# Inverting the 16x16 diagonal blocks of a delta rule on VectorE by forward substitution, in place of doubled powers on TensorE

## The reference

```python
decay = jnp.exp(jnp.where(causal, gc[..., :, None] - gc[..., None, :], -jnp.inf))
kk = jnp.einsum("nbhcd,nbhed->nbhce", kc, kc)
a_mat = jnp.where(strict, bc[..., :, None] * kk * decay, 0.0) + jnp.eye(CHUNK, dtype=f32)
rhs = jnp.concatenate([vc * bc[..., None], kc * (bc * jnp.exp(gc))[..., None]], axis=-1)
sol = lax.linalg.triangular_solve(a_mat, rhs, left_side=True, lower=True)
...
def step(state, xs):
    v_new = u_n - jnp.einsum("bhck,bhkv->bhcv", w_n, state)
    o = (jnp.einsum("bhck,bhkv->bhcv", q_n * jnp.exp(g_n)[..., None], state)
         + jnp.einsum("bhce,bhev->bhcv", attn_n, v_new))
    state = state * jnp.exp(gl_n)[..., None, None] + jnp.einsum("bhck,bhcv->bhkv", kt_n, v_new)
```

## Time and profile before

| what | us |
|---|---|
| median of 3 runs | 1206.51 |
| lowest and highest | 1205.79, 1206.98 |
| the profiled execution, its own time | 1207.03 |
| its span, first to last instruction | 1205.3 |
| PE busy | 1180.6 (98%) |
| DVE, ACT, POOL busy | 744.6, 597.4, 102.2 |

### The profile page before, as it was taken

One profiled execution on the slowest core, in us unless ns is written; L12 is line 12 of the kernel. 1 busy time (PEld: TensorE's weight loads), 2 busy tenths in 40 slices (PEclk: granted clock), 3 DMA queues, 4 the chain that ended last, 5 costly groups with the idle time before them and its releaser, 6 DMA issues.

```text
span 1205.3 us, 20514 instructions
## 1 busy us (share of the span) xinstructions
PE 1180.6 (98%) x8276; PEld 1100.7 (91%) x8276; DVE 744.6 (62%) x897; ACT 597.4 (50%) x804; POOL 102.2 (8%) x159
## 2 busy tenths in 40 slices
PE   7999999999999999999999999999999999999997
PEld 6998899999888999988999998789999989999875
DVE  5867556555867797763565544565766466554455
ACT  4675444346455675653444433455464355443342
POOL 5310101001010000000000000100400010000011
PEclk8999999999999999999999999999999999999999
DMA  8744343445554675656476555465475548655541
GB/s 223 221 127 153 105 140 106 140 140 198 187 191 140 187 216 174 195 189 187 137 224 195 182 175 195 139 211 172 141 228 191 159 141 268 193 175 175 203 135 63
DMA packets 156019, 208.57 MB, mean 173 GB/s; under 512 B 8608, under 2 KB 127405, under 8 KB 155949
## 3 DMA queue, kind: packets, MB, share of 16 engines
q1 hardware_dynamic: 152781, 198.92, 52.4%
q10 hardware_dynamic: 3072, 8.65, 2.2%
q0 software_dynamic: 96, 0.01, 0.1%
HBM read 206.50 MB, written 1.05 MB: 172 GB/s over the span
## 4 chain that ended last, share of the span: by engine, by line
PE 92%; DVE 3%; ACT 2%; POOL 1%; issue 1%; DMA 1%; POOLq 0%; DVEq 0%; SPq 0%; ACTq 0%
PE ACCP L774 27%; PE ACCP L776 27%; PE ACCP L775 27%; PE SMP L925 3%; PE SMP L918 2%; PE SMP L774 2%; PE SMP L776 2%; PE SMP L775 2%; ACT HI L1399 1%; DVE LO L1899 1%; POOL STAT L651 1%; DMA PRE_GAIN<-in_norm_mix_dram 1%; DVE XS L1935 0%; POOL STAT L650 0%; PE ACCP L895 0%
## 5 line engine op out<-in xcount | busy, mean ns | idle before, releaser
L1899 DVE TENSOR_TENSOR LO<-RAW,HI 128x1024 fp32r<-128x1024 f32 x367 | 437.6, 1231 | 244.9 <-ACT HI L1399 243.8
L1399 ACT ACTIVATE HI<-RAW 128x1024 fp32r<-128x1024 f32 x366 | 368.5, 1053 | 226.9 <-PE ACCP L776 206.1
L774 PE MATMUL ACCP<-XH,HI 128*128 128x256 f32 x1536 | 437.8, 285 | 1.9 <-DVE XL L1944 1.9
L775 PE MATMUL ACCP<-XL,HI 128*128 128x256 f32 x1536 | 435.8, 284 | 0.0
L776 PE MATMUL ACCP<-XH,LO 128*128 128x256 f32 x1536 | 435.8, 284 | 0.0
L774 PEld LDWEIGHTS ACCP<-XH,HI 128*128 128x128 f32 x1536 | 296.0, 193 | 2.3 <-DVE LO L1899 2.2
L775 PEld LDWEIGHTS ACCP<-XL,HI 128*128 128x128 f32 x1536 | 296.0, 193 | 0.0
L776 PEld LDWEIGHTS ACCP<-XH,LO 128*128 128x128 f32 x1536 | 296.0, 193 | 0.0
L774 PE MATMUL ACCP<-HI,HH 128*128 128x512 f32 x264 | 105.0, 398 | 0.0
L776 PE MATMUL ACCP<-HI,HL 128*128 128x512 f32 x264 | 104.6, 396 | 0.0
L775 PE MATMUL ACCP<-LO,HH 128*128 128x512 f32 x264 | 104.6, 396 | 0.0
(11 more groups left out here) (388 smaller groups left out, 1536.0 us busy)
## 6 DMA issues: line engine op xcount, KB each, us to landing
RAW<-in_w_in_dram SPq DMA_DIRECT2D x104, 512.0 KB, 4.4
RAW<-in_w_up_dram SPq DMA_DIRECT2D x44, 512.0 KB, 4.5
RAW<-in_ffn_w_gate_dram SPq DMA_DIRECT2D x44, 512.0 KB, 4.4
RAW<-in_ffn_w_up_dram SPq DMA_DIRECT2D x44, 512.0 KB, 4.6
RAW<-in_ffn_w_down_dram SPq DMA_DIRECT2D x44, 512.0 KB, 4.1
RAW<-in_w_down_dram SPq DMA_DIRECT2D x22, 512.0 KB, 4.1
RAW<-in_w_out_dram SPq DMA_DIRECT2D x8, 512.0 KB, 4.2
RAW<-in_w_mkv_dram SPq DMA_DIRECT2D x8, 512.0 KB, 5.0
```

Of the source, the lines that this page charges most:

```text
L774: pe.matmul(dst, lhs[0], rhs[0], start=start, stop=False)
L775: pe.matmul(dst, lhs[0], rhs[1], start=False, stop=False)
L1399: act.activation(HI[:, n % RING, half_of(half)], RAW[:, n % RAWS, half, :], ACT.Copy).then_inc(hi_ready, 1)
L1899: dve.tensor_tensor(LO[:, s, c], RAW[:, n % RAWS, half, :], HI[:, s, c].bitcast(f32), ALU.subtract).then_inc(lo_ready[s], 1)
```

## The change

The products Dt to P8 leave PE, with the copies that ACT, DVE and POOL make for them. Instead:

1. SP writes the 64 diagonal 16x16 blocks of L to a scratch tensor in DRAM: 8 DMAs, each of 16 partitions with 8 pieces of 64 bytes. They stand between the loads of foxv.0 and foxv.1.
2. After the load of foxv.1, SP waits for them and loads the scratch tensor into DIAG_L: one block a partition, 64 partitions of 1 KB.
3. DVE waits for that and solves all 64 blocks at once by forward substitution: 15 columns, two operations a column (a product of n x m elements, and a subtraction), n = j + 1, m = 15 - j. Each waits for the one before (`link`). The result in DIAG_T is the transposed inverse.
4. SP stores DIAG_T to a second scratch tensor, loads gate_c.0, and places the blocks into MP with 8 DMAs of 64-byte pieces. PE waits for these (diag_placed) ahead of `T16`.

POOL zeroes MP and sets up DIAG_T, where it built the mask DIAG16 before. The arena, the stretch of SBUF that most tiles share, is declared ahead of the small tensors COL, FCONV, IDENT and so on, so that its start is a multiple of 64 bytes.

```diff
-        DL, MAT, MA, MB, MC, ME, MP = (at(f"delta_{n}", 24 + 4 * i, [P, NT, HEADS, P])
-                                        for i, n in enumerate(["L", "AT", "A", "B", "C", "E", "P"]))
+        DL, MAT, MA, MB = (at(f"delta_{n}", 24 + 4 * i, [P, NT, HEADS, P]) for i, n in enumerate(["L", "AT", "A", "B"]))
+        ME, MP = (at(f"delta_{n}", 44 + 4 * i, [P, NT, HEADS, P]) for i, n in enumerate(["E", "P"]))
+        DIAG_L, DIAG_T, DIAG_TERM = (at(f"diag_{n}", 40 + i, [N_DIAG, 16, 16]) for i, n in enumerate(["L", "T", "term"]))
+        diag_l, diag_t = (nc.dram_tensor(f"scratch_diag_{n}", (NT * HEADS, P // 16, 16, 16), f32) for n in "lt")
...
-            load_t("foxv", w["w_in"], C_FV)
+            for j in range(2):
+                load("foxv", Turn(j), t_block(w["w_in"], C_FV, j))
+                if j == 0:
+                    for t in range(NT):
+                        small_is_taken(sp, f"kk{t}")
+                    for g in range(P // 16):
+                        sp.dma_start(diag_l[:, g, :, :].rearrange("q r c -> r q c"), diagonal(DL, g)).then_inc(diag_written, 16)
+            sp.wait_ge(diag_written, 16 * (P // 16))
+            sp.dma_start(DIAG_L[:, :, :].rearrange("b r c -> b (r c)"), diag_l[:, :, :, :].rearrange("q g r c -> (q g) (r c)")).then_inc(diag_loaded, 16)
+            sp.wait_ge(diag_solved, 1)
+            sp.dma_start(diag_t[:, :, :, :].rearrange("q g c r -> (q g) (c r)"), DIAG_T[:, :, :].rearrange("b c r -> b (c r)")).then_inc(diag_stored, 16)
...
+                    if g == "c" and j == 0:
+                        sp.wait_ge(diag_stored, 16)
+                        sp.wait_ge(diag_zeroed, 3)
+                        for i in range(P // 16):
+                            sp.dma_start(diagonal(MP, i), diag_t[:, i, :, :].rearrange("q c r -> c q r")).then_inc(diag_placed, 16)
...
-            for t in range(NT):
-                pe.wait_ge(D_ready, t + 1)
-                turn_four(f"Dt{t}", lambda h: MA[:, t, h, :])
-            t_half("foxqk", 0, XH, XL)
-            for t in range(NT):
-                small_is_taken(pe, f"Dt{t}")
-                four(f"D2_{t}", lambda h: (MB[:, t, h, :], MA[:, t, h, :]))
...
+            for j in range(3):
+                t_half("foxqk", j, XH, XL)
...
-            for t in range(NT):
-                small_is_taken(pe, f"P8_{t}")
+            pe.wait_ge(diag_placed, 16 * (P // 16))
+            for t in range(NT):
                 turn_four(f"T16_{t}", lambda h: MP[:, t, h, :])
...
+            dve.wait_ge(diag_loaded, 16)
+            dve.wait_ge(diag_zeroed, 3)
+            for j in range(15):
+                n, m = j + 1, 15 - j
+                below = DIAG_L[:, n:16, j:n].rearrange("b r o -> b o r").broadcast_to([N_DIAG, n, m])
+                solved = DIAG_T[:, 0:n, j:n].broadcast_to([N_DIAG, n, m])
+                rest = DIAG_T[:, 0:n, n:16]
+                link(dve.tensor_tensor(DIAG_TERM[:, 0:n, 0:m], below, solved, ALU.mult))
+                ins = dve.tensor_tensor(rest, rest, DIAG_TERM[:, 0:n, 0:m], ALU.subtract)
+                if j < 14:
+                    link(ins)
+            ins.then_inc(diag_solved, 1)
```

More of the change, by code:

```diff
@@ L134 @@
 SMALL += ["gTq0", "gTq1", "gTk0", "gTk1", "gTv0", "gTv1", "gcol", "grow0", "grow1", "gFq0", "gFq1", "gFk0", "gFk1"]
-SMALL += ["kk0", "kk1", "kq0", "kq1", "z0", "z1", "z2", "z3", "Dt0", "Dt1", "D2_0", "D2_1", "D2t_0", "D2t_1"]
-SMALL += ["P2_0", "P2_1", "D4_0", "D4_1", "D4t_0", "D4t_1", "rc0", "rc1", "rc2", "rc3", "P4_0", "P4_1"]
-SMALL += ["D8_0", "D8_1", "P8_0", "P8_1", "so0", "so1", "T16_0", "T16_1", "fTq0", "fTq1", "fTk0", "fTk1"]
+SMALL += ["kk0", "kk1", "kq0", "kq1", "z0", "z1", "z2", "z3", "rc0", "rc1", "rc2", "rc3", "so0", "so1", "T16_0", "T16_1", "fTq0", "fTq1", "fTk0", "fTk1"]
 SMALL += ["Z16_0", "Z16_1", "Tt32_0", "Tt32_1", "fS0", "fS1a", "fS1b", "Z32_0", "Z32_1", "T32_0", "T32_1"]
@@ L221, in build @@
         XS = sb("XS", [P, NT, DM])
-        COL = [sb(f"COL{i}", [P, n]) for i, n in enumerate(COL_N)]
-        FCONV = sb("FCONV", [P, CONV_N])
+        ARENA = 86 * 1024
+        arena = sb("arena", [P, ARENA // 4])
+        base = nc.sbuf_base - ARENA
         IDENT = sb("IDENT", [P, P])
@@ L233, in build @@
         TRI = UPTO[:, 0, :]
+        COL = [sb(f"COL{i}", [P, n]) for i, n in enumerate(COL_N)]
+        FCONV = sb("FCONV", [P, CONV_N])
         STAT = sb("STAT", [P, 384])
@@ L374, in build @@
         post_sq, tap_done, dve_mix = sems("post_sq tap_done dve_mix")
+        diag_zeroed, diag_written, diag_loaded, diag_solved, diag_stored, diag_placed = sems(
+            "diag_zeroed diag_written diag_loaded diag_solved diag_stored diag_placed")
         ln_mean, ln_sq, ln_ready = sems("ln_mean ln_sq ln_ready")
@@ L578, in _, with diagonal @@
             load_t("foxqk", w["w_in"], C_FQ)
-            load_t("foxv", w["w_in"], C_FV)
+            def diagonal(m, g):
+                part = slice(16 * g, 16 * g + 16)
+                return m[part, :, :, part].rearrange("r t h c -> r (t h) c")
+            for j in range(2):
[9 more added lines that the diff above has]
+            sp.dma_start(diag_t[:, :, :, :].rearrange("q g c r -> (q g) (c r)"), DIAG_T[:, :, :].rearrange("b c r -> b (c r)")).then_inc(diag_stored, 16)
             for g, branch, wo in (("c", 2, "w_oc"), ("a", 0, "w_oa"), ("b", 1, "w_ob")):
@@ L582, in _ @@
                     load_f("gz", w["w_in"], C_GZ)
-                load_f(f"gate_{g}", w["w_in"], C_GATE + DM * branch)
+                for j in range(4):
+                    load(f"gate_{g}", Turn(j), f_block(w["w_in"], C_GATE + DM * branch + 256 * j))
+                    if g == "c" and j == 0:
[3 more added lines that the diff above has]
+                            sp.dma_start(diagonal(MP, i), diag_t[:, i, :, :].rearrange("q c r -> c q r")).then_inc(diag_placed, 16)
                 for j in range(2):
@@ L723, in _ @@
             pool.memset(ONES, 1.0).then_inc(masks_ready, 1)
+            pool.memset(MP[:, :, :, :], 0.0).then_inc(diag_zeroed, 1)
+            pool.memset(DIAG_T[:, :, :], 0.0).then_inc(diag_zeroed, 1)
+            pool.wait_ge(diag_zeroed, 2)
+            pool.memset(DIAG_T[:, :, :].rearrange("b c r -> b (c r)")[:, 0:256:17], 1.0).then_inc(diag_zeroed, 1)
             lo_of(ON_POOL_CONV)
@@ L729, in _ @@
                 small_is_taken(pool, f"kk{t}")
-                pool.tensor_tensor(MA[:, t], DL[:, t], every(DIAG16[:, :], HEADS), ALU.mult).then_inc(D_ready, 1)
             heads_root(1, 1.0 / DH)
-            for b, last in ((16, "D8"), (32, "Z16"), (64, "Z32")):
+            for b, last in ((16, ""), (32, "Z16"), (64, "Z32")):
                 for t in range(NT):
-                    small_is_done(pool, f"{last}_{t}")
+                    if last:
+                        small_is_done(pool, f"{last}_{t}")
                     pool.tensor_tensor(MA[:, t], DL[:, t], every(LEVEL[b][:, :], HEADS), ALU.mult).then_inc(level_ready, 1)
@@ L1047, in _ @@
                 rest_sums(h)
[L1048 to L1060, removed]
+            for j in range(2):
+                t_half("foxv", j, XH, XL)
             pe.wait_ge(stick_ready, 1)
@@ L2060, in _ @@
             dve.scalar_tensor_tensor(out=SP_[:, :, :], in0=Z[:, :, :], scalar=-1.0, in1=Z[:, :, :], op0=ALU.mult, op1=ALU.max).then_inc(keep_abs, 1)
[L2062 to L2070, removed]
+            dve.wait_ge(diag_loaded, 16)
[10 more added lines that the diff above has]
+            ins.then_inc(diag_solved, 1)
             split_ahead("foxqk", Turn(0))
-            take_small("D2_1", MC[:, 1], by_head(small("D2_1")))
             dve.wait_ge(keep_ln, 1)
@@ L2076, in _ @@
             dve.tensor_tensor(SP_[:, :, SEQ:SEQ + P], SP_[:, :, SEQ:SEQ + P], every(BEFORE[:, :], HEADS), ALU.mult).then_inc(keep_ready, 1)
-            take_small("D2t_1", ME[:, 1], by_head(small("D2t_1")))
             split_ahead("foxqk", Turn(1))
[L2080 to L2088, removed]
             split_ahead("foxqk", Turn(2))
-            take_small("D4t_1", MB[:, 1], by_head(small("D4t_1")))
             def stick_arg(h):
@@ L2101, in _ @@
                 stick_arg(h)
-            for t in range(NT):
-                factor(4, t)
             heads_norm(1, XS, 2 * HW)
             heads_scale(1, lambda t: HT[:, t, :], 8)
-            split_ahead("foxv", Turn(0), (0,))
-            take_small("D8_1", MC[:, 1], by_head(small("D8_1")))
-            split_ahead("foxv", Turn(0), (1,))
+            split_ahead("foxv", Turn(0))
             split_ahead("foxv", Turn(1))
-            for t in range(NT):
-                factor(8, t)
             y_split(0, ("so0", "so1"), lambda g: (YH[:, 2 * g:2 * g + 2, :], YL[:, 2 * g:2 * g + 2, :], by_head(small(f"so{g}"), SEQ)))
```

28 lines of the change are left out of this document (2 added, 26 removed).

## The result

| | median, us | lowest to highest | ratio to before, 95% interval |
|---|---|---|---|
| before | 1206.21 | 1205.79 to 1206.98 | |
| after | 1187.72 | 1186.72 to 1190.55 | 0.9852 [0.9839, 0.9866] |

The account below looks back on a forecast made before the run. TensorE, busy for 98% of the span, was taken as the bound. Gross gain 14.1 less a 0.4 us wait gave 13.7, so 1207.03 became 1193.3, the median 1192.8, stated as 1193.0; range 1191.4 to 1198.0.

Parts of the forecast that it names:

- The shift of the arena costs nothing: Arena's new start: no cost, argued from 512-column operations taking 682 ns on X and XS outside it, 690 on SP_ inside.
- Gross gain 14.1: PE in the delta rule: removed stretches of 13.71 us plus 0.39 for three blocks that follow a block.
- Dt: Removed products ahead of foxqk.0: worth nothing, since the wait there for ACT's copy just grows by about 0.8 us.
- The landing: DIAG_L's load on SP's queue: issued at about 104.9, behind 512 KB landing at 108.3, it lands at 108.9.
- rival 1: The chain is late: landing or solve slips, PE waits 2 to 6 us at rc0, say 4; 1196.5 us, chance 0.20.
- one full small landing more: Upper bound on DIAG_L's landing: 108.3 + 3.8 = 112.1, with a PE wait at rc0 of 3.6 us.
- The solve, 7.2 us: DVE's 30 linked operations at 0.195 us each plus 1.02 ns an element, 1360 elements; bounds 5 and 14 us.
- Rival 2, the column read: DVE reading DIAG_L down a column costs two to four times, solve grows 0.7 to 2.1 us; 1194.2, chance 0.12.
- keep_ready: DVE's signal that PE needs at rc0: comes at 121.6 against PE's arrival at 121.2, a wait of 0.4 us.
- stick_ready: After foxv.1, ACT's exponential ends 5.0 us after foxv.0, foxv.1 covers 5.44: slack 0.4 us, no wait.
- Rivals 3, 4 and 5: Later waits at stick_ready or norms, 1195, 0.07; slow small operations, 1223, 0.05; waits replace PE's removed stretches, 1206.5, 0.03.
- The sum: Whole kernel: gross gain 14.1 less 0.4 of wait at rc0, 13.7 us.

Follow-up runs that it names:

- e5: Kernel before with COL and FCONV declared behind the arena, so the arena has an offset of 0 from HI; 1199.74 us.
- e12: Changed kernel with 96 bytes ahead of its arena, the old offset from HI, so the delta rule's change alone; 1193.62 us.
- e7: Changed kernel with the load of DIAG_L issued ahead of foxv.1 instead of behind it; 1185.38 us.
- e9: Changed kernel with XH and XL 32 bytes off HI and LO, arena at 0 mod 256 from HI, COL0 ahead of the arena; 1176.41 us.
- e11: Changed kernel with XH and XL 64 bytes off HI and LO, arena at 0 mod 256 from HI, COL0 ahead of the arena; 1177.02 us.
- e2: Changed kernel with FCONV declared ahead of the arena, which then starts 32 past a multiple of 64 bytes; 1192.19 us.
- e3: Changed kernel with XH and XL moved to 32 mod 64 by pads, arena then 64 off HI mod 256; 1178.03 us.
- e4: Changed kernel with HI and LO moved to 32 mod 64 by pads, arena then 32 off HI mod 256; 1179.18 us.
- e6: Changed kernel with XH and XL 32 bytes off HI and LO, arena at 128 mod 256 from HI; 1178.64 us.
- e10: e9 plus the load of DIAG_L ahead of foxv.1 and ACT's copy to SV after Z's first half; 1172.28 us.
- e1: Kernel before with FCONV declared behind the arena, which then starts at a multiple of 64 bytes; 1203.65 us.

## Why the prediction was wrong, point by point

**The step that failed most** is the last sentence ahead of the sum: "The shift of the arena costs nothing". It was argued from two rows of DVE, on which the shift indeed does nothing (682 and 691 ns after). But the arena also holds HH, the stationary operand of 792 products of 512 columns, and PE is the engine that bounds the kernel. The missing term is 792 x 7.6 ns = 6.0 us, and 0.67 for the products with MH and YH; e5 measured 6.3, and e12 lies 5.9 above the changed kernel. I costed an edit at nothing by looking at an engine with slack and not at the one without.

**Gross gain 14.1.** Right. From foxqk.0 to the end of the delta rule PE gained 13.55 - 1.85 = 11.7 us with a wait of 2.31 in it, so 14.0 without. Between whole kernels with the same arena offset and no wait: e5 to e7, 1199.74 - 1185.38 = 14.4. Dt was worth nothing, as forecast: the wait for ACT's SV copy grew from 0.62 to 1.57, by 0.95 where 0.8 was said. The three blocks took 16.6 us to the last product's end, against 5.57 + 5.44 + 5.44 = 16.45.

**The landing.** DIAG_L landed at 109.0 and I had said 108.9, but this is luck. All that comes ahead of it ran 1.85 us earlier than in the trace of before. From its own issue the load took 6.1 us, where 108.9 - 104.9 = 4.0 was taken. The mis-sized term is the landing of the half megabyte ahead of it: 4.0 us in the sum, 6.4 measured. The 4.0 is the median of 19 loads, and the sum gave it to one that is not like the median. The trace of before has this very load, the second half of foxv.1, issued at 104.29:

```profile
RAW<-in_w_in_dram SPq DMA_DIRECT2D x1, 512.0 KB, 6.1
```

So "no landing in this stretch is far off its 4.0", with which rival 1 was held small, was a misreading: 104.29 + 6.1 = 110.4, and the wait at rc0 would have come out near 2. The 0.6 us for DIAG_L behind it were 0.2, and the small writes landed after 1.8 and not 3.8, which changed nothing. The bound from above, "one full small landing more", was wide enough. This is rival 1, *the chain is late*, with 2.31 us of wait instead of its 4, one microsecond for one microsecond, as it says.

**The solve, 7.2 us.** 109.03 to 116.33, 7.30. The pitch model (0.195 plus 1.02 ns an element) holds: the pair of 64 elements starts 0.29 and 0.25 apart.

**Rival 2, the column read.** Each pair has equal counts, the first reading DIAG_L at a stride of 64 bytes, the second not: 0.26 and 0.22 us at 64 elements and 0.17 and 0.17 at 15. So the strided read costs at most 40 ns an operation, some 0.4 us over the fifteen (the two also differ in what they broadcast), where two to four times the element cost would have been 0.7 to 2.1. The Trainium skill's rule of 16-byte lines in "SBUF — State Buffer", Door 1, has at most this much behind it here.

**The rest of the chain.** keep_ready came at 121.79, forecast 121.6. PE arrived at 119.5 and not 121.2, as everything ahead ran earlier, and DIAG_L did not land earlier with it: hence 2.31 and not 0.4. stick_ready: ACT's exponential ended at 142.11 and PE came at 142.54 without waiting, the forecast slack of 0.4. The placements were issued from 119.17 on and landed after 3.0; T16, at 150.9, did not wait. Rivals 3, 4 and 5 did not happen; a small operation of the solve takes 0.17 to 0.26 us, not 1.24.

**The sum** for the delta rule was 13.7 and measured 12.5 (e12), 11.7 in the trace; what is missing is the landing, some 2 us of wait. What put the result outside the range was the arena: with it at its old place (e12) the time is 1193.6.

## What to carry to other kernels

When a change moves a tensor in SBUF, list the products that read it and compare their pitch before and after over hundreds of products. Nothing waits, PE's busy share stays at 98%, and 7 ns a product were 6 us here. A small load that a chain waits for belongs ahead of the big ones in its queue, and where it stands behind one, take that one's own landing from the trace and not the median of its kind. A cost of nothing must be argued from the engine that bounds the kernel.

## What the runs showed of the hardware that was not expected

The pitch of an fp32r product depends on the offset between its two operands in a partition. In the table it is where HH or XH starts less where HI starts; HI and LO, and XH and XL, lie multiples of 256 apart, and the slices that the products take start at multiples of 512 bytes in their tensors. HI is the moving operand of the products of 512 columns and the stationary one of those of 256. Each value is the length of unbroken stretches over their count, at a granted clock of 1.00:

| offset, bytes mod 256 | 512 columns: HI,HH or HI,XH | 256 columns: XH,HI or HH,HI |
|---|---|---|
| 0 | 226.7 to 227.1 ns (after, e5, e9, e11) | 120.1 (before, after, e5) |
| 32 | 233.1 to 233.3 (e2, e3, e4) | 116.8 (e3, e6, e9; e4 and e10 but for one phase each at 117.9), 117.8 (HH,HI in e2) |
| 64 | 233.3 to 233.5 (e1, e3, e11) | 117.9 and 113.4 (e11), 117.8 (e1), 117.4 (e3) |
| 96 | 234.3 (before, e12) | 120.0 (before) |
| 128 | 232.4 (e6) | 118.7 (e6) |

So of the offsets tried, products of 512 columns are fastest at 0, and those of 256 columns at 32 and 64; at 96 the latter gain nothing, which is why the 720 products of 256 columns that read HH or YH ran at 120 ns before and after. It is the relation that counts: e3 moved XH by 32 bytes and e4 moved HI by 32 and XH by 64, with the same pitches but for that one phase. For 256 columns the offset is not all: at 32 HH,HI takes 116.7 in e4 and 117.8 in e2. The Trainium skill, "SBUF — State Buffer", Who interferes with whom, gives TensorE two read ports, one for the moving operand and one for the weight load, and calls them independent. Here the measurement decides: they are independent as ports, perhaps, but a product's pace hangs on where the two operands lie to each other. The mechanism is not shown by any run here, nor why e4, e10 and e11 change pitch within one execution, nor a modulus above 256: e9 has the arena at 256 mod 512 from HI and is as fast as at 0, and larger offsets were not varied on purpose.
